# Attention scores issued in fours at the head of a softmax step, after the exps have given back their PSUM banks

## The reference

```python
o_a = dilated_mixture(...)   # kind A: 6 heads of 64, causal with dilated windows, bias
o_b = diff_attention(...)    # kind B: 4 heads, two score maps of 32 columns each:
                             #   softmax(q1 k1) - lam * softmax(q2 k2), times v
o_c = causal_attention(...)  # kind C: 6 heads, q and k of 64 + 32 (rotary) columns
h = layer_norm(ALPHA * x + concat(o_a, o_b, o_c) @ w_o)
```

## Time and profile before

| | |
|---|---|
| median of 3 runs | 2960.75 us (2959.88 to 2961.22) |
| the profiled execution | 2960.39 us |
| its span on the core | 2958.6 us |
| granted clock of PE | 0.999 |
| PE / DVE / ACT busy | 99% / 65% / 44% |
| attention, layer 0 | 45 to 236 us of the span |
| attention, layer 1 | 681.6 to 872.6 us |

### The profile page before, as it was taken

One profiled execution on the slowest core, in us unless ns is written; L12 is line 12 of the kernel. 1 busy time (PEld: TensorE's weight loads), 2 busy tenths in 40 slices (PEclk: granted clock), 3 DMA queues, 4 the chain that ended last, 5 costly groups with the idle time before them and its releaser, 6 DMA issues.

```text
span 2958.6 us, 39561 instructions
## 1 busy us (share of the span) xinstructions
PE 2919.7 (99%) x16598; PEld 2485.9 (84%) x16598; DVE 1927.5 (65%) x2830; ACT 1288.0 (44%) x1996; POOL 262.6 (9%) x207
## 2 busy tenths in 40 slices
PE   9999999999999999999999999999999999999998
PEld 7767899977667999978999998888888888889997
DVE  4576576664657676776546556667777794576675
ACT  4554354444535354463334244444333335254444
POOL 0232000020231000010000001010101021000000
PEclk9999999999999999999999999999999999999999
DMA  5113442322124423212121223121212133322232
GB/s 191 45 58 157 185 160 92 108 100 77 44 93 166 171 100 107 95 70 72 62 81 52 71 74 110 48 99 47 99 51 90 47 121 128 121 82 98 100 107 79
DMA packets 45058, 285.32 MB, mean 96 GB/s; under 512 B 5135, under 2 KB 5663, under 8 KB 19408
## 3 DMA queue, kind: packets, MB, share of 16 engines
q1 hardware_dynamic: 42480, 269.77, 25.5%
q0 software_dynamic: 2400, 13.02, 1.2%
HBM read 276.98 MB, written 5.79 MB: 96 GB/s over the span
## 4 chain that ended last, share of the span: by engine, by line
PE 89%; DVE 5%; ACT 4%; POOL 1%; issue 1%; DMA 0%; DVEq 0%; SPq 0%; POOLq 0%; ACTq 0%
PE ps L858 18%; PE ps L860 18%; PE ps L859 18%; PE ps L1112 9%; PE ps L1114 9%; PE ps L1113 9%; PE ps L1030 2%; PE ps L1043 1%; PE ps L1057 1%; DVE wlo L2010 1%; PE ps L957 1%; ACT whi L1374 1%; ACT SQL L1416 1%; PE ps L941 1%; POOL tmp_a L2780 1%
## 5 line engine op out<-in xcount | busy, mean ns | idle before, releaser
L2010 DVE TENSOR_TENSOR wlo<-wraw,whi 128x1536 fp32r<-128x1536 f32 (+2 forms) x221 | 425.3, 1924 | 237.9 <-ACT whi L1374 237.9
L1374 ACT ACTIVATE whi<-wraw 128x1536 fp32r<-128x1536 f32 (+2 forms) x221 | 353.3, 1599 | 458.1 <-PE ps L860 386.2
L858 PE MATMUL ps<-A1h,whi 128*128 128x512 f32 x1024 | 412.1, 402 | 8.1 <-DVE A1l L2031 7.3
L860 PE MATMUL ps<-A1h,wlo 128*128 128x512 f32 x1024 | 400.3, 391 | 0.0
L859 PE MATMUL ps<-A1l,whi 128*128 128x512 f32 x1024 | 400.1, 391 | 0.0
L1112 PE MATMUL ps<-A1h,whi 128*128 128x256 f32 (+1 forms) x836 | 245.7, 294 | 2.4 <-DVE wlo L2010 1.6
L1114 PE MATMUL ps<-A1h,wlo 128*128 128x256 f32 (+1 forms) x836 | 244.4, 292 | 0.0
L1113 PE MATMUL ps<-A1l,whi 128*128 128x256 f32 (+1 forms) x836 | 244.3, 292 | 0.0
L858 PEld LDWEIGHTS ps<-A1h,whi 128*128 128x128 f32 x1024 | 193.6, 189 | 52.0 <-issue 11.5
L860 PEld LDWEIGHTS ps<-A1h,wlo 128*128 128x128 f32 x1024 | 192.9, 188 | 41.2
L859 PEld LDWEIGHTS ps<-A1l,whi 128*128 128x128 f32 x1024 | 193.3, 189 | 38.9 <-issue 2.2
(11 more groups left out here) (524 smaller groups left out, 7176.8 us busy)
## 6 DMA issues: line engine op xcount, KB each, us to landing
wraw<-wstream SPq DMA_DIRECT2D x159, 1024.0 KB, 4.8
MW<-wstream SPq DMA_DIRECT2D x34, 1024.0 KB, 6.8
wraw<-wstream SPq DMA_DIRECT2D x42, 768.0 KB, 4.3
wraw<-wstream SPq DMA_DIRECT2D x34, 640.0 KB, 3.9
wraw<-wstream SPq DMA_DIRECT2D x4, 960.0 KB, 4.7
TB<-gd POOLq DMA_DIRECT2D x1, 2560.0 KB, 13.3
X<-xT SPq DMA_DIRECT2D x4, 512.0 KB, 7.0
sx<-X POOLq DMA_DIRECT2D x1, 2048.0 KB, 7.6
```

What stands on the lines that cost most here:

```text
L858: mm(o, l[0], r[0], start=start, stop=False)
L860: return mm(o, l[1], r[0], start=False, stop=stop)
L1374: act(whi[i_ % 2][:, 0:n], wraw[i_ % 2][:, 0:n], ACT.Copy, bias=0.0, scale=1.0).then_inc(ev("hi", i_).by(act_whi), 1)
L2010: tt(wlo[i_ % 2][:, 0:n], wraw[i_ % 2][:, 0:n], raw(whi[i_ % 2][:, 0:n]), SUB).then_inc(ev("lo", i_).by(dve_wlo), 1)
```

## The change

Three edits. In the loop of steps `exps` now comes before `scores`, and `scores` comes at every second step in B (before: at every step) and at every fourth in A and C (before: every second). What it issues is four matmul groups: in B both maps of both heads of a pair for one block; in A and C both heads for two blocks, i and i + 1. And the first panel of the output projection is worked in tiles 0 and 1 together, then tile 2.

```diff
-WO_TILES = ((0, ((0, 1, 2),)), (3, ((0,), (1,), (2,))), (6, ((0,), (1,))))
+WO_TILES = ((0, ((0, 1), (2,))), (3, ((0,), (1,), (2,))), (6, ((0,), (1,))))
...
-        if step < n and (here == "B" or step % 2 == 0):
-            put("scores", *items[step])
         if 0 <= step - 1 < n:
             put("exps", *items[step - 1])
+        if step < n and step % (2 if here == "B" else 4) == 0:
+            put("scores", *items[step])
...
                     if what == "scores":
                         kd, h, i = x
-                        n = 128 * (i + 1)
+                        four = [(h_, i, m) for h_ in (h, h + 1) for m in range(2)] if kd == "B" else [(h_, i_, 0) for i_ in (i, i + 1) for h_ in (h, h + 1)]
...
-                        for h_, m in ((h, 0), (h, 1)) if kd == "B" else ((h, 0), (h + 1, 0)):
-                            b = AB.hold("s", l, kd, h_, i, m)
+                        for h_, i_, m in four:
+                            b, n = AB.hold("s", l, kd, h_, i_, m), 128 * (i_ + 1)
                             q, k = qk_of(kd, h_, m)
                             e.wait_ge(b.before)
-                            last = mm(b.ap[:, 0:n], q[:, 128 * i:128 * i + 128], k[:, 0:n], start=True, stop=kd != "C")
+                            last = mm(b.ap[:, 0:n], q[:, 128 * i_:128 * i_ + 128], k[:, 0:n], start=True, stop=kd != "C")
...
                         if kd == "C":
-                            for h_ in (h, h + 1):
-                                b = AB.of("s", l, kd, h_, i, 0)
+                            for h_, i_, _ in four:
+                                b, n = AB.of("s", l, kd, h_, i_, 0), 128 * (i_ + 1)
                                 q, k = qk_of(kd, h_, 1)
-                                mm(b.ap[:, 0:n], q[:, 128 * i:128 * i + 128], k[:, 0:n], start=False, stop=True).then_inc(b.full.by(product), 1)
+                                mm(b.ap[:, 0:n], q[:, 128 * i_:128 * i_ + 128], k[:, 0:n], start=False, stop=True).then_inc(b.full.by(product), 1)
```

## The result

The changed kernel takes 2977.17 us (median of 4 runs, 2976.84 to 2978.35) against 2960.52 us of the kernel before in the same job: a ratio of 1.0057 (95% interval 1.0039 to 1.0074), 16.65 us slower. The forecast was 2969, 8 us slower, with a range from 2953 to 2976. The direction came as said and so did the waits in B; the loss is twice the one forecast, and the time lies 1.2 us above the range.

A forecast was written before the change was run, and what follows sets the result against it. PE bounds the kernel, busy 2919.7 of 2958.6 us. Per layer B gains 6.3 against 7.0 of waits (0.7 lost), A and C lose 3.5: 4.2, in all 8.4 on the 2960.75 median, 2969 us; range 2953 to 2976.

The forecast's parts named there:

- B's slots: Scores in attention steps 0 to 15: a four takes a pair's time, eight pairs a layer go, 6.3 us a layer gained.
- The rival that four groups would not run side by side: Scores in B: slots of 1.3 to 1.5 pairs add 2 to 3 us a layer, 2974 us; chance 0.10.
- B's waits: Five places a layer in steps 0 to 16 where PE waits for a bank an exp gives back; 7.0 us.
- Step 4: In B: the transpose waits for a bank whose exp is queued behind a split on DVE; 2.1 us.
- Step 8: In B: the next tile waits for the bank of an exp ending at 81.41; about 1.3 us.
- Step 14: In B: the tile waits for an exp's bank, DVE's work in front being paced by a tile; 1.1 us.
- Step 16: Start of A: the ckv tile waits for the bank of an exp ending at 118.17; about 2.0 us.
- A and C: Steps 16 to 63: no slots saved, later transposes and P times V cost 0 to 5 us a layer; 3.5 taken.
- step 32: In A: the tile of 163.31 also waits, for an exp ending at 164.80; 1.5 us.
- step 53: In C: the third output projection tile, regrouped, waits for an exp ending at 206.34; 1.6 us.
- Releases come in time: Rival, all attention: B's waits halve, A's and C's are given back; 4.0 us a layer faster, 2953 us; chance 0.24.
- Gain and waits cancel: Rival, all attention: B's 6.3 us against all waits at half to two thirds; 2956 to 2966 us; chance 0.22.

The follow-up runs named there:

- Experiment 5: Fours in B only, items of steps 4 and 5 in pairs, against the kernel before (2960.42 us): at the step's head 2955.83, at its tail 2958.34 us.
- the kernel with short fours: Against the kernel before: fours only for A's query blocks 0 and 1 (steps 16, 24, 32), the rest pairs, old output grouping; 2971.43 against 2960.11 us.
- the kernel with B at the tail: Against the kernel before: fours in B only, behind the even step's transpose and tile matmuls; 2956.91 against 2960.08 us, again 2957.51 against 2960.42.

## Why the prediction was too low

**B's slots: right.** 16 slots, eight passes each. Where no wait falls into one it is as long as a pair's (0.44, 0.64, 0.86 and 1.07 us against 0.42, 0.63, 0.84 and 1.06). The rival that four groups would not run side by side is refuted. The Trainium skill gives 3.07x for four row tiles against one ("TensorE: Matmul & The Clock Gate", the section on measured speedup); no run here has one group alone, and from two to four this trace shows no loss.

**B's waits: right, better than PE's idle time shows.** The prediction counted from start to start, so layer 1 has to be read the same way. Step 4: 2.1 us forecast, 2.3 measured (709.61 - 706.44, less a slot). Step 8: 1.3 and 1.2, before the transpose and not before the tile. Step 10: 0.5 and 0.2. Step 14: 1.1 and 0.9, inside the four. Step 16: 2.0 and 2.4. Sum: 7.0 and 7.0. That the sums agree so well is in part luck: by the prediction's own figures steps 4 and 8 come to 2.2 and 1.5. Up to the ckv tile of step 16 layer 1 became 72.36 - 70.85 = 1.5 us longer, where 0.7 was forecast; 0.4 of the difference is the second pair of A, which now stands ahead of that tile.

**A and C: here the step failed.** The prediction said "From 0 (all is given back) to 5 us ...; I take 3.5". Behind the ckv tile layer 1 became 7.1 - 1.5 = 5.6 us longer, above even the upper bound. The two places that were worked out came as said: step 32 with 0.59 + 0.85 us of idle time against 1.5, step 53 with 1.46 against 1.6. The places that nobody looked for made the rest: the fours of steps 28 and 48 took 1.8 us each longer than the same fours elsewhere (3.48 against 1.71; 3.35, from 843.01 to 846.36, against 1.52, from 864.55 to 866.07), and PE waited 0.64 us at step 31, 1.14 at step 39 and 0.51 at step 47. The upper bound counted places found and added "two or three like them", instead of asking for how many of the 12 fours the last bank comes late. On the other side stands a gain that the sum put at 0 and kept for the range, "at most 0.2 us for each of the 12 merges": it came. A's four at step 24 took 0.85 us (791.36 to 792.21) against 0.42 + 0.63 for two pairs, and C's long four at step 60 took 3.21 us (871.32 to 874.53) against 1.49 + 1.92; if all twelve gave as much, 2.4 us a layer were saved in A and C, an estimate. Without it the miss would have been larger.

**The clock: missing.** No term had it, since the earlier trace rows show 1.00 in both layers. The two falls of layer 0, 3.4 us by the windows and 3.2 by the difference of the layers, are a fifth of the whole loss.

**The sum, both layers** (forecast, then measured): up to the ckv tile of step 16 +1.4 and +3.0; behind it +7.0 and +11.2; clock 0 and +3.2; ahead of layer 0, 0 and -0.7. The measured column adds to 16.7. Of the 8.3 us that were missing, 4.2 are A and C, 3.2 the clock and 1.6 the way up to step 16. The sign that the prediction named for being right, attention at 193 to 197 us in each layer, was missed too: 198.1 and 201.7.

**The rivals.** "Releases come in time" was the wrong guess for the whole, though the point named for it holds: "where the exp is released before PE reaches the transpose, B gives its full" gain. Experiment 5 made that true at one step, and the kernel became faster than before. "Gain and waits cancel" is how B alone comes out in time (+1.2 us); in a layer without a fall of the clock it gains 0.9 us. The reason given against the first rival, that exps of steps 4, 8 and 16 are held up by DVE's splits and copies whatever lies ready, was right: in the changed kernel the split on DVE ran from 59.31 to 61.60 and the exp behind it at 62.04. The Trainium skill warns of PSUM pressure where row tiles stand side by side ("TensorEngine Tiling (Array Packing)", Gotcha 1). This trace agrees for B, with 2.24 us at the worst place.

**What stays open.** Which release ended the waits inside the fours of A and C was read from single rows and not tested by an experiment of its own. What decides whether the clock falls behind a given wait was not found.

## What to carry to other kernels

A slot saved on the busy engine is only worth what is left after its buffers' releases: go through the ring for *every* place where more are held at once, and let the bound of the cost grow with their number, not with the places found first. Read a wait from the start of one row to the start of the next, since idle time misses what falls inside a row. Where merging pays in most places and one place eats it, undo it there: one four of eight put back into pairs moved this kernel from +1.2 to -4.6 us. And on an engine that is otherwise never idle, price a new wait of 1 to 2 us with the clock that may fall behind it, here mostly 1.5 to 1.6 us each time it did (once 1.2, once some 3).

## What the runs showed of the hardware that was not expected

- **The granted clock falls behind short waits, and not always.** Behind 2.24 us of idle PE it fell in layer 0 and not in layer 1 of two kernels; in the kernel with short fours it fell behind the wait of step 16 in layer 1 and not in layer 0 (0.81 against 1.00 over 9 us); and of two executions of one kernel one had it (0.82) and one had not (1.00). By the lengths of two layers of one kernel a fall mostly costs 1.5 to 1.6 us, in the kernel with B at the tail 1.2 in layer 0 (184.95 against the 183.77 of the execution without a fall); by the windows it is 1.7, once 3.2. It shows in whole runs too: of eleven runs of the kernel with B at the tail, those with a mean clock of 0.999 took 2955.6 and 2956.2 us, those with 0.998 took 2956.8 to 2957.5 and those with 0.997 took 2958.8 to 2960.4. And it isn't chance alone: all ten runs with fours in B at the head stand at 0.998, ten of the eleven with pairs at steps 4 and 5 at 0.999. So one profile can't tell whether a wait has this price, and a difference of 1 to 3 us between two profiles can be this alone.
- **It need not be a new wait.** In the kernel with only the order changed, a wait of 1.76 us in a later stage, which the kernel before has too (1.74 us), drew a fall. Windows over that stretch, before and with the order changed:

```profile
1345.00:1350.00 5.00, 3.26 (x19) 3.26 (x20) 4.20 (x6) 2.09 (x4) 0.00 (x0) 1.00 0.14 59
```

```profile
1345.00:1350.00 5.00, 3.64 (x13) 3.64 (x14) 4.21 (x5) 2.09 (x5) 0.00 (x0) 0.71 0.06 26
```

- **Four 32-row groups of fp32 matmuls cost what two cost**: 0.93 us for eight passes of 384 columns, 0.91 for four.
- **A matmul row can hide a wait.** The four at 753.06 counts as busy for 1.84 us, where the same four without a wait has 1.14; the wait of 0.41 us shows only between its weight loads.
